# Second up product: four of sixteen weight remainders by an accumulating transfer

## The reference

```python
def conv_gated_ffn(h, w_up, conv_w, conv_b, w_down):
    u = h @ w_up
    up_ = jnp.pad(u, ((0, 0), (1, 1), (0, 0)))
    u = up_[:, :-2] * conv_w[0] + up_[:, 1:-1] * conv_w[1] + up_[:, 2:] * conv_w[2] + conv_b
    gate, val = jnp.split(u, 2, axis=-1)
    return (jax.nn.silu(gate) * val) @ w_down
```

## Time and profile before

| | before |
|---|---|
| median of 3 runs | 2138.94 us |
| lowest and highest | 2136.22 and 2138.98 us |
| span of the profiled execution | 2138.7 us |
| busy: TensorE, VectorE, ScalarE, GpSimd | 99%, 80%, 55%, 2% |
| DMA, mean of the span | 184 GB/s |

### The profile page before, as it was taken

How to read it: one execution, slowest core, us unless ns; L and a number is a source line. 1 busy time by engine, 2 the same in 40 slices (tenths; PEclk the granted TensorE clock), 3 DMA queues, 4 the chain that set the end, 5 groups by cost and what they waited for, 6 DMA issues and landing times.

```text
span 2138.7 us, 27894 instructions
## 1 busy us (share of the span) xinstructions
PE 2123.2 (99%) x9739; PEld 1762.8 (82%) x9739; DVE 1701.1 (80%) x2489; ACT 1166.1 (55%) x1521; POOL 49.8 (2%) x59
## 2 busy tenths in 40 slices
PE   9999999999999999999999999999999999999999
PEld 7897888888888888888889878888888888888887
DVE  5899977888888867864555557569999999999877
ACT  6556665444544444544466436555666666655454
POOL 1000000000000000000000033000000000000000
PEclk9999999999999999999999999999999999999999
DMA  7665355666666666566555644456666666656655
GB/s 225 198 176 170 120 181 151 213 188 186 201 202 191 191 197 214 189 215 194 157 164 166 173 125 148 147 178 187 188 195 191 190 193 189 196 178 197 214 198 177
DMA packets 216080, 393.31 MB, mean 184 GB/s; under 512 B 13519, under 2 KB 58137, under 8 KB 215739
## 3 DMA queue, kind: packets, MB, share of 16 engines
q1 hardware_dynamic: 215819, 391.13, 59.5%
q10 hardware_dynamic: 176, 1.06, 0.1%
HBM read 390.04 MB, written 2.10 MB: 183 GB/s over the span
## 4 chain that ended last, share of the span: by engine, by line
PE 84%; DVE 9%; issue 4%; ACT 2%; DVEq 0%; ACTq 0%; POOL 0%; POOLq 0%
PE ps L625 22%; PE ps L627 22%; PE ps L626 22%; PE ps L938 4%; PE ps L940 4%; PE ps L939 4%; DVE w_lo L2014 2%; DVE val_T L2067 2%; DVE gate_T L2067 1%; PE ps L663 1%; ACT w_hi L1343 1%; DVE cv L2126 0%; DVE stage L2861 0%; DVE stage L2869 0%; PE ps L1123 0%
## 5 line engine op out<-in xcount | busy, mean ns | idle before, releaser
L2014 DVE TENSOR_TENSOR w_lo<-raw,w_hi 128x1024 fp32r<-128x1024 f32 (+2 forms) x724 | 864.2, 1205 | 300.4 <-ACT w_hi L1343 293.4
L1343 ACT ACTIVATE w_hi<-raw 128x1024 fp32r<-128x1024 f32 (+2 forms) x724 | 748.4, 1041 | 598.6 <-PE ps L627 469.5
L625 PE MATMUL ps<-w_hi,hT_hi 128*128 128x512 f32 (+2 forms) x1904 | 744.2, 391 | 3.5 <-DVE w_lo L2014 2.8
L627 PE MATMUL ps<-w_hi,hT_lo 128*128 128x512 f32 (+2 forms) x1904 | 734.7, 386 | 0.0
L626 PE MATMUL ps<-w_lo,hT_hi 128*128 128x512 f32 (+2 forms) x1904 | 734.4, 386 | 0.0
L625 PEld LDWEIGHTS ps<-w_hi,hT_hi 128*128 128x128 f32 x1904 | 358.1, 188 | 78.2 <-DVE w_lo L2014 6.5
L627 PEld LDWEIGHTS ps<-w_hi,hT_lo 128*128 128x128 f32 x1904 | 357.9, 188 | 67.8
L626 PEld LDWEIGHTS ps<-w_lo,hT_hi 128*128 128x128 f32 x1904 | 358.3, 188 | 64.3
L625 PE MATMUL ps<-w_hi,aT_hi 128*128 128x512 f32 x544 | 212.0, 390 | 1.0 <-DVE w_lo L2014 1.0
L626 PE MATMUL ps<-w_lo,aT_hi 128*128 128x512 f32 x544 | 211.7, 389 | 0.0
L627 PE MATMUL ps<-w_hi,aT_lo 128*128 128x512 f32 x544 | 211.6, 389 | 0.0
(11 more groups left out here) (393 smaller groups left out, 1914.5 us busy)
## 6 DMA issues: line engine op xcount, KB each, us to landing
raw<-in_w_up SPq DMA_DIRECT2D x264, 512.0 KB, 3.9
raw<-in_w_down SPq DMA_DIRECT2D x172, 512.0 KB, 4.6
raw<-in_w_gate SPq DMA_DIRECT2D x88, 512.0 KB, 4.3
raw<-in_w_in SPq DMA_DIRECT2D x80, 464.0 KB, 3.5
raw<-in_w_out SPq DMA_DIRECT2D x64, 512.0 KB, 3.9
raw<-in_w_in SPq DMA_DIRECT2D x64, 256.0 KB, 3.3
raw<-in_w_in SPq DMA_DIRECT2D x24, 448.0 KB, 3.6
raw<-in_w_uq SPq DMA_DIRECT2D x9, 512.0 KB, 3.9
```

The lines of the kernel that those rows point to most:

```text
L625: pe.matmul(o, xh, wh, start=first, stop=False)
L627: mm = pe.matmul(o, xl, wh, start=False, stop=last)
L1343: act.activation(w_hi[:, s, :kc, :width], raw[:, s, :kc, :width], ACT.Copy).then_inc(hi_ready, 1)
L2014: dve.tensor_tensor(w_lo[:, s, :kc, :width], raw[:, s, :kc, :width], w_hi[:, s, :kc, :width].bitcast(F32), ALU.subtract).then_inc(lo_ready, 1)
```

## The change

In each of the ten turns of the loop, tiles 4, 6, 9 and 11 (`ADDED`) get their remainder in another way. ScalarE, behind the rounding of `raw` into `w_hi`, writes the negated rounding of `raw` into `w_lo`. GpSimd waits for that (`negated`) and issues a transfer that adds `raw` (512 KB in SBUF) onto `w_lo`; its landing counts up `lo_added` of the slot. VectorE leaves these four tiles out, and the remainder ahead of each counts `lo_ready` up by two. TensorE waits for `lo_added` before tiles 4, 6, 9 and 11; SyncE waits for it before it loads tiles 8, 10, 13 and 15, which use the same slots' `raw`. The orders of all other work stay; where `hi_tiles` and `lo_tiles` stood in the loops, `up2_hi` and `up2_lo` stand with the same bounds. `pool_seen` and `sp_seen` are counted and nobody waits for them.

```diff
+ADDED = [4, 6, 9, 11]
...
+        negated, pool_seen, sp_seen = sem("negated"), sem("pool_seen"), sem("sp_seen")
+        lo_added = [sem(f"lo_added{s}") for s in range(RING)]
...
             with sp.Fori(1, FB) as j:
-                load_block(T_FF2, 16 * j, w_up2, [2] * 8, cols(j))
-                load_block(T_FF2 + 8, 16 * j, w_up2, [2] * 8, cols(j + FB))
+                for n in range(16):
+                    if n - RING in ADDED:
+                        sp.wait_ge(lo_added[(T_FF2 + n) % RING], 16 * j)
+                        sp.sem_inc(sp_seen)
+                    load(T_FF2 + n, 16 * j, w_up2, 2 * (n % 8), cols(j + FB * (n // 8)))
...
+            with pool.Fori(1, FB) as j:
+                for i, n in enumerate(ADDED):
+                    pool.wait_ge(negated, 4 * j - 3 + i)
+                    pool.sem_inc(pool_seen)
+                    pool.dma_start(w_lo[:, (T_FF2 + n) % RING], raw[:, (T_FF2 + n) % RING], accum_op=ALU.add).then_inc(lo_added[(T_FF2 + n) % RING], 16)
...
             with pe.Fori(1, FB) as j:
-                pe.wait_ge(gemm_free[0], G_FF2 + j)
-                ff_tiles(T_FF2, 16 * j, 0, 0, 8)
-                pe.wait_ge(gemm_free[1], G_FF2 + j)
-                ff_tiles(T_FF2 + 8, 16 * j, 1, 0, 8)
+                for half in range(2):
+                    pe.wait_ge(gemm_free[half], G_FF2 + j)
+                    for n in range(8 * half, 8 * half + 8):
+                        if n in ADDED:
+                            pe.wait_ge(lo_added[(T_FF2 + n) % RING], 16 * j)
+                        gemm_tile(T_FF2 + n, 16 * j, H, 2 * (n % 8), pair(half), n % 8 == 0, n % 8 == 7)
...
+            def up2_hi(j, lo, hi):
+
+                for n in range(lo, hi):
+                    split_hi(T_FF2 + n, 16 * j)
+                    if n in ADDED:
+                        act.activation(w_lo[:, (T_FF2 + n) % RING], raw[:, (T_FF2 + n) % RING], ACT.Copy, scale=-1.0).then_inc(negated, 1)
+
             with act.Fori(1, FB) as j:
-                hi_tiles(T_FF2, 16 * j, 0, 2)
+                up2_hi(j, 0, 2)
                 center2(j - 1, 0)
...
-            def split_lo(c0, step):
+            def split_lo(c0, step, tiles=1):
...
                 dve.tensor_tensor(w_lo[:, s, :kc, :width], raw[:, s, :kc, :width],
-                                  w_hi[:, s, :kc, :width].bitcast(F32), ALU.subtract).then_inc(lo_ready, 1)
+                                  w_hi[:, s, :kc, :width].bitcast(F32), ALU.subtract).then_inc(lo_ready, tiles)
...
+            def up2_lo(j, lo, hi):
+
+                for n in range(lo, hi):
+                    if n not in ADDED:
+                        split_lo(T_FF2 + n, 16 * j, 2 if n + 1 in ADDED else 1)
+
             with dve.Fori(1, FB) as j:
-                lo_tiles(T_FF2, 16 * j, 0, 2)
+                up2_lo(j, 0, 2)
                 taps2(j - 1, 0)

```

More of the change, by code:

```diff
@@ L1975, in _ @@
             hi_upto(T_FF2 + 16)
+            def up2_hi(j, lo, hi):
[3 more added lines that the diff above has]
+                        act.activation(w_lo[:, (T_FF2 + n) % RING], raw[:, (T_FF2 + n) % RING], ACT.Copy, scale=-1.0).then_inc(negated, 1)
             with act.Fori(1, FB) as j:
-                hi_tiles(T_FF2, 16 * j, 0, 2)
+                up2_hi(j, 0, 2)
                 center2(j - 1, 0)
-                hi_tiles(T_FF2, 16 * j, 2, 3)
+                up2_hi(j, 2, 3)
                 copy2(j - 1, 1)
-                hi_tiles(T_FF2, 16 * j, 3, 6)
+                up2_hi(j, 3, 6)
                 silu2(j - 1)
-                hi_tiles(T_FF2, 16 * j, 6, 8)
+                up2_hi(j, 6, 8)
                 center2(j - 1, 1)
-                hi_tiles(T_FF2, 16 * j, 8, 11)
+                up2_hi(j, 8, 11)
                 copy2(j, 0)
                 hidden_hi(j - 1)
-                hi_tiles(T_FF2, 16 * j, 11, 16)
+                up2_hi(j, 11, 16)
             done[0] = T_DN2
@@ L2882, in hidden_lo @@
                                   aT_hi_flat[:, bass.ts(j, 4 * SEQ)].bitcast(F32), ALU.subtract).then_inc(aT_ready, 1)
+            def up2_lo(j, lo, hi):
+                for n in range(lo, hi):
+                    if n not in ADDED:
+                        split_lo(T_FF2 + n, 16 * j, 2 if n + 1 in ADDED else 1)
             with dve.Fori(1, FB) as j:
-                lo_tiles(T_FF2, 16 * j, 0, 2)
+                up2_lo(j, 0, 2)
                 taps2(j - 1, 0)
-                lo_tiles(T_FF2, 16 * j, 2, 3)
+                up2_lo(j, 2, 3)
                 for n in range(4):
-                    lo_tiles(T_FF2, 16 * j, 3 + n, 4 + n)
+                    up2_lo(j, 3 + n, 4 + n)
                     value_strips(j - 1, val_T, n)
-                lo_tiles(T_FF2, 16 * j, 7, 8)
+                up2_lo(j, 7, 8)
                 taps2(j - 1, 1)
                 product2(j - 1)
-                lo_tiles(T_FF2, 16 * j, 8, 12)
+                up2_lo(j, 8, 12)
                 hidden_lo(j - 1)
```

## The result

| | before | changed |
|---|---|---|
| median, 4 runs each | 2138.93 us | 2203.77 us |
| lowest and highest | 2136.22 and 2138.98 | 2193.19 and 2209.06 |
| span of the profiled execution | 2138.7 us | 2201.5 us |
| ratio, 95% interval | | 1.030, 1.0272 to 1.0327 |

The change costs 64.8 us, 3.0%. The forecast was 2173 us with a range of 2136 to 2212, so the sign and the place were right, and the forecast loss of 34 us was about half of the measured 65.

A forecast was written before the change was run, and what follows sets the result against it. TensorE, busy 99%, was taken as the bound, stopping only 0.29 us a turn for VectorE. Late additions at tiles 6 and 11 lose 3.7 us a turn, 37 in ten, less 2.9: +34, 2173 us, range 2136 to 2212.

The forecast's parts named there:

- What can be given back: 2.9 us: TensorE's stops at tile 8 for VectorE's remainder, 0.29 us a turn; with VectorE relieved they go, 2.9 us in ten turns.
- ScalarE's four negations at nothing: Four added negated roundings a turn on ScalarE, 1.0 us each, hidden by idle time or slack, so no loss.
- The margins: Time from negation's end to the tile's start: 5.9 us at tile 4, 5.3 at 6, 4.8 to 5.9 at 9, 3.8 at 11.
- The later tile of a pair decides: Stops at tiles 4 and 6, or 9 and 11, do not add; tiles 6 and 11 set the loss, 1.1 and 2.6 us.
- D = 6.4: Time from the negation's end on ScalarE to the addition's landing as TensorE sees it: 4.65 + 1.6 + 0.1 = 6.4 us.
- second pass: The accumulating transfer also reads its target, which takes one more pass over the tile on the DMA engines, 1.6 us.
- the meeting with loads: The addition runs among loads, so its base was 4.65 us, midway between median and slowest load, not the fastest's 3.4.
- A turn loses its stops, and no more: Loop loss per turn is only the overruns at tiles 6 and 11, 3.7 us, less 0.29 given back at tile 8.
- The margin of tile 11 shrinks by 0.4 us behind a held load: Tile 10's load waits for an addition's landing, delaying its rounding and ScalarE's next work; 4 us in ten turns, upper side.
- The rival that it fits: If negation's end to landing takes 3.8 us or less, no tile is late: 2136 us; rival "not slower", chance 0.17.
- My bound below, 3.5: Lowest time from negation's end to landing: the fastest 512 KB load, 3.4 us, with a 0.1 step between engines.
- The rival of full DMA engines: DMA share 92%, additions and loads hold each other up, or an addition costs two transfers: +80 us, 2219; chance 0.13.

The follow-up runs named there:

- eight_first: The kernel before with tile 8's remainder moved on VectorE ahead of the previous turn's product: 2135.34 us, ratio 0.9987.
- plain_small: The changed kernel with 32 KB loads in the loop and a plain transfer in place of the accumulating one: 2135.99 us, one run.
- only_9: The changed kernel with the added transfer for tile 9 alone, the other three remainders by VectorE as before: 2146.22 us, one run.
- four_nine: The changed kernel with added transfers for tiles 4 and 9 only: 2147.27 us, ratio 1.0048.
- six_nine: The changed kernel with added transfers for tiles 6 and 9 only: 2142.85 us, one run.
- filled: The changed kernel with 8, 4 and 6 extra 128-column matmuls right ahead of the waits at tiles 6, 9 and 11: 2196.57 us, ratio 1.0292.
- small_loads: The changed kernel with loop loads of 32 KB in place of 512 KB, all waits and accumulating transfers kept: 2150.57 us, one run.
- paced: The changed kernel with loads 11 and 12 held until TensorE is done with tiles 6 and 7: 2208.35 us, ratio 1.0321.

## Why the prediction was right in sign and short in size

- *What can be given back: 2.9 us.* Right, and shown twice: eight_first and plain_small both bring the loop to the sum of its matmuls, within 0.3 us. In the changed kernel the stop at tile 8 is gone as well.
- *ScalarE's four negations at nothing.* Right as far as seen: where the chains fitted (plain_small), nothing else was late. ScalarE was busy 31.2 us a turn and VectorE 37.1, forecast 31.6 and 36.7.
- *The margins.* Right within 0.1 us: 3.74 for 3.8 at tile 11, 5.8 for 5.9 at tile 4, and at tile 9 both ends of the forecast were seen, 4.75 in only_9 and 5.8 in four_nine. In six_nine tile 6 stopped by 0.5 us at chains of 5.7, so its margin was 5.2, forecast 5.3.
- *The later tile of a pair decides.* Right for 4 and 6: tile 4 stopped by 2.6 us in ten turns, tile 6 by 20.5. It held for 9 and 11 too, though the sum had put the whole stop at tile 11: tile 9's chain was so long that tile 9 stopped in five turns, by 10.2 us, and in those turns tile 11's stop was at least 0.9 us less than its chain less 3.7, and in one turn it was gone.
- *D = 6.4.* Too small: 7.1 on average. On free engines the terms are right together by luck: fastest transfer 3.4, second pass 1.6 and hops 0.1 make 5.1, and 5.0 was measured, but out of other parts. A plain transfer within SBUF lands after 2.8, less than the fastest load; from the end of the negation to the start of GpSimd's issue alone 0.6 us pass; and the 1.6 for the second pass is 1.2 of work on the DMA engines and 0.3 of GpSimd's instruction. What was too small was the meeting with loads, for which 4.65 in place of 3.4 was to stand, 1.25 us. It was worth 0.7, 2.4, 3.9 and 1.5 us at the four tiles. It was one number for all four, and it left out that the additions lengthen each other, by held loads or by their own work. Net of the 2.9 us, the stops cost 46 us where the sum had 34.
- *A turn loses its stops, and no more.* This term was missing: behind a stop the clock can be at its lower level, and slow matmuls hold 17.3 us. The sum, 49.0 + 17.3 - 2.9 (the stops given back), is 63.4 of the 64.3 us. That is where the time went; what the loop would take at the full clock is less sure, since filled gave back only 6.8 of it.
- *The margin of tile 11 shrinks by 0.4 us behind a held load.* Kept on the upper side, and not seen in the changed kernel: where tile 9 had not stopped, the margin was 3.65 to 3.78.
- *The rival that it fits.* Excluded by small_loads: 5.0 us on free engines against 3.8 at tile 11. My bound below, 3.5, was that of a plain transfer, 3.4 in plain_small.
- *The rival of full DMA engines.* Their share in the loop was 75% in place of the 92% worked out, in part since the loop is longer: the same work in the 438 us of before would be 86%. The mechanism of this rival, additions and loads holding each other up, is at work although the engines are not full, and its size lies between the forecast's and this rival's.

By the fit of the Trainium skill for a transfer issued by GpSimd (DMA: Bandwidth & Descriptors, Anatomy of one DMA — SWDGE (gpsimd) path) the estimate was 3.2 us; the plain one took 2.8 to 3.3 on nearly free engines, with a median of 2.9. The same page of the Trainium skill says that an accumulate reads its destination and writes it later (Rules for kernel authors); the 2.65 us on each DMA engine against 1.42 for the plain one agree with that.

What stays open: how much of the 2.1 us that the chains spend above 5.0 is bunching and how much the traffic itself. paced shows that spreading two loads shortens tile 9's landing by 2.3 us, without the loop being faster; six_nine shows that a held load alone does not lengthen it. Nor is it shown why some long stops were followed by slow matmuls and others not. In the changed kernel nine of 23 stops with over 1 us from start to start were, one of 2.18 among them, while one of 2.69 was not.

## What to carry to other kernels

Before moving work off a nearly full engine, work out how long the bounding engine really stops for it; here it was 0.3 us in 43.8, and one reordered line gave it back. Work moved to a transfer changes from busy time to latency. In a ring of four slots it must fit into three tiles less all that stands ahead of it on its engines, and the landing to count with is the one it gets among the other transfers, at its own place in the turn. And a stop of the bounding engine can cost more than its length.

## What the hardware showed that I had not expected

- A stop of TensorE with 2.5 us from start to start was followed in eight of ten cases by six to eight matmuls at the lower clock, some 1.6 us more; one of 1.31 us in none of ten.
- An accumulating transfer of 512 KB within SBUF lands 4.4 us after the start of its issue, a plain one after 2.8, both on nearly free DMA engines; among loads the accumulating one took up to 9.9. It holds each DMA engine for 2.65 us in place of 1.42.
- GpSimd's issuing instruction took 0.85 us for the accumulating transfer and 0.53 for the plain one.
- From the end of the negation on ScalarE to the start of GpSimd's issue passed 0.6 us, with a wait and the counting of `pool_seen` between them; VectorE, which has the wait alone, starts within 0.1 us of a rounding's end.
